# Two float32 blocks on one Trainium2 core: the high and low parts of the weights become slices of one tensor that begin 16 bytes into it, and every SBUF tensor behind them starts 32 bytes later

## What is computed

```
def swiglu(h, w_in, w_out):
    gate, up = jnp.split(h @ w_in, 2, axis=-1)
    return (jax.nn.silu(gate) * up) @ w_out
...
px = modulate(rms_norm(x, g_pre_mix[layer]), sh_m, sc_m) @ w_in[layer]
pc = modulate(rms_norm(ctx, g_pre_mix[layer]), csh_m, csc_m) @ w_in[layer]
...
mix_x = jnp.concatenate([att_x, ml_x], axis=-1) @ w_out[layer]
...
h = h + 0.5 * swiglu_2(rmsnorm(h, ffn1_norm[l]), ffn1_w_gate[l], ffn1_w_up[l], ffn1_w_down[l])
u = rmsnorm(h, mix_norm[l])
(aq, ak, av, gq, gk, gv, gr, g_low, gate_a, gate_b) = jnp.split(u @ w_in[l], offsets, axis=-1)
```

## The kernel before, in words

| operand | read by | start, mod 256 |
|---|---|---|
| `hi`, `lo` (any tile) | all large products | 0 |
| `mixH`, `mixL`, any k, 256 columns | `wout` (L2397), `bra`, `brb`, `wout2`, `gu2` | 192 |
| `g_high`, `g_low`, 256 columns | `dn0`, `dn2` | 192 |
| `g_high`, `g_low`, 272 columns | `dn1` | 192, 0, 64, 128 in turn with k |
| `n_high`, `n_low`, 258 columns | `gu0` | 192 |
| `n_high`, `n_low`, 272 columns | `gu1`, part of `in2k` | 192 |
| `n_high`, `n_low`, the 256 frames behind the 16 meta tokens | rest of `in2k`, `in2g` | 0 |
| `n5H`, `n5L`, 256 columns (L2133) | first block's projections | 128 |
| `row1` (weights of L2071, 2 moving columns) | modulation vectors | 224 |

## Time and profile before

### The profile page before, as it was taken

One profiled execution on the slowest core, in us unless ns is written; L12 is line 12 of the kernel. 1 busy time (PEld: TensorE's weight loads), 2 busy tenths in 40 slices (PEclk: granted clock), 3 DMA queues, 4 the chain that ended last, 5 costly groups with the idle time before them and its releaser, 6 DMA issues.

```text
span 963.9 us, 19405 instructions
## 1 busy us (share of the span) xinstructions
PE 950.4 (99%) x7543; PEld 882.2 (92%) x7543; DVE 639.9 (66%) x990; ACT 494.6 (51%) x762; POOL 69.1 (7%) x100
## 2 busy tenths in 40 slices
PE   8999999999999999999999999999999999999997
PEld 3776778899999999899999999999998999999997
DVE  4888886687666675765555546665777766666554
ACT  3765647655444544554444434644566555454531
POOL 0012002200000021000000000200120100000000
PEclk9999999999999999999999999999999999999999
DMA  9972437547556795266666744663345557667741
GB/s 361 400 259 89 132 132 242 164 166 216 174 176 183 206 320 158 68 197 175 180 181 179 222 118 127 211 191 110 111 131 163 167 156 235 193 197 210 218 142 44
DMA packets 189183, 176.06 MB, mean 183 GB/s; under 512 B 7312, under 2 KB 177824, under 8 KB 188752
## 3 DMA queue, kind: packets, MB, share of 16 engines
q1 hardware_dynamic: 183456, 154.29, 53.3%
q0 software_dynamic: 4960, 17.64, 5.2%
q10 hardware_dynamic: 720, 3.49, 0.9%
HBM read 174.32 MB, written 1.05 MB: 182 GB/s over the span
## 4 chain that ended last, share of the span: by engine, by line
PE 91%; DVE 6%; ACT 2%; issue 1%; POOL 0%; DVEq 0%; ACTq 0%; POOLq 0%
PE acc L2004 24%; PE acc L2006 24%; PE acc L2005 24%; PE acc L2397 2%; PE acc L2100 1%; PE acc L2202 1%; PE acc L2204 1%; PE acc L2203 1%; PE wk L2063 1%; PE wk L2004 1%; PE acc L2133 1%; PE wk L2006 1%; PE wk L2005 1%; DVE lo L1142 1%; PE wk L2701 1%
## 5 line engine op out<-in xcount | busy, mean ns | idle before, releaser
L1142 DVE TENSOR_TENSOR lo<-raw,hi 128x1024 fp32r<-128x1024 f32 (+1 forms) x259 | 330.9, 1288 | 205.7 <-ACT hi L620 205.4
L620 ACT ACTIVATE hi<-raw 128x1024 fp32r<-128x1024 f32 (+1 forms) x260 | 283.2, 1099 | 126.0 <-PE acc L2006 120.4
L2004 PE MATMUL acc<-n_high,hi 128*128 128x272 f32 (+3 forms) x1016 | 292.1, 288 | 0.4 <-DVE hbuf L1670 0.4
L2005 PE MATMUL acc<-n_low,hi 128*128 128x272 f32 (+3 forms) x1016 | 289.1, 285 | 0.0
L2006 PE MATMUL acc<-n_high,lo 128*128 128x272 f32 (+3 forms) x1016 | 289.1, 285 | 0.0
L2004 PEld LDWEIGHTS acc<-n_high,hi 128*128 128x128 f32 (+1 forms) x1016 | 192.2, 189 | 2.8 <-issue 1.4
L2005 PEld LDWEIGHTS acc<-n_low,hi 128*128 128x128 f32 (+1 forms) x1016 | 192.3, 189 | 0.5
L2006 PEld LDWEIGHTS acc<-n_high,lo 128*128 128x128 f32 (+1 forms) x1016 | 192.2, 189 | 0.2
L2004 PE MATMUL acc<-g_high,hi 128*128 128x256 f32 (+1 forms) x528 | 148.4, 281 | 0.0
L2006 PE MATMUL acc<-g_high,lo 128*128 128x256 f32 (+1 forms) x528 | 148.1, 281 | 0.0
L2005 PE MATMUL acc<-g_low,hi 128*128 128x256 f32 (+1 forms) x528 | 147.9, 280 | 0.0
(11 more groups left out here) (424 smaller groups left out, 1248.9 us busy)
## 6 DMA issues: line engine op xcount, KB each, us to landing
raw<-in_w_in SPq DMA_DIRECT2D x52, 512.0 KB, 3.9
raw<-in_w_ffn_in SPq DMA_DIRECT2D x44, 512.0 KB, 4.0
raw<-in_ffn_w_gate SPq DMA_DIRECT2D x44, 512.0 KB, 3.8
raw<-in_ffn_w_up SPq DMA_DIRECT2D x44, 512.0 KB, 3.8
raw<-in_ffn_w_down SPq DMA_DIRECT2D x32, 704.0 KB, 4.6
stage<-in_w_late POOLq DMA_DIRECT2D x24, 512.0 KB, 4.9
raw<-in_w_ffn_out SPq DMA_DIRECT2D x16, 704.0 KB, 5.8
raw<-in_w_out SPq DMA_DIRECT2D x16, 512.0 KB, 3.8
```

Source lines behind the costliest of these rows:

```text
L620: act.activation(hi[:, j, 0:width], raw[:, j, 0:width], ACT.Copy).then_inc(hi_ready, 1)
L1142: dve.tensor_tensor(lo[:, j, 0:width], raw[:, j, 0:width], hi[:, j, 0:width].bitcast(F32), ALU.subtract).then_inc(lo_ready, 1)
L2004: pe.matmul(out_, wH, xH, start=start, stop=False)
L2005: pe.matmul(out_, wH, xL, start=False, stop=False)
```

## The change

`hi` and `lo` are no longer two tensors. One tensor `split` of 2 x 4 x 1408 + 8 float32 (45088 bytes) takes their place, and `hi` and `lo` are views of it that leave 4 elements (16 bytes) free at its start and 4 at its end:

```
-        hi = sbuf(root, "hi", [P, RING, SLOT], F32R)
-        lo = sbuf(root, "lo", [P, RING, SLOT], F32R)
+        split = sbuf(root, "split", [P, 2 * RING * SLOT + 8], F32R)
+        hi, lo = (split[:, 4 + n * RING * SLOT:4 + (n + 1) * RING * SLOT].rearrange("p (j w) -> p j w", j=RING) for n in range(2))
```

## The result

The changed kernel took 981.06 us (median of 4 runs; 977.49 to 985.74), the kernel before beside it 969.48 us (median of 4 runs; 965.49 to 973.77). The ratio is 1.013, with a 95% interval of 1.0094 to 1.0166: slower by about 12 us. The forecast was 980 us. The profiled execution took 984.56 us, its span 982.8.

What follows compares the result with a forecast made beforehand. TensorE, busy 99% of the span, was taken to bound the kernel through the distance between matmul starts. The 967.4 us median plus 12.5 us for 2496 matmuls, all else zero, gave 980 us; 8-in-10 range 952 to 992.

Steps and rivals of the forecast that it cites:

- What bounds the kernel: Whole kernel: time is the number of matmuls times the distance between starts; the change acts only through that distance.
- (a): ACT and DVE accesses to hi and lo start 16 bytes later, some transfers 32: counted at nothing, hidden behind TensorE.
- (b): Large products: moving operands start 32 bytes later, weights 16; 2496 matmuls lose 5 ns each, 12.5 us (0 to 20).
- The row chosen for the price: Price per matmul for the 256-column groups at 192: taken from n5L, 281 against 276 ns, so +5 ns.
- the likeness with 258 columns: Moving operands: 256 columns from 224 touch 17 pieces of 64 bytes, as 258 columns do; at worst +8 ns.
- the comparison of rows 3 and 4: Equal-width matmuls by moving start mod 256: 276 to 277 ns at 192, 283 at 0, 281 at 128.
- (c): Weight loads, starting at 16 instead of 0: no change taken, with 7 ns for each load kept as a rival.
- The step beside it: Weight loads at 256 columns: the load, 112 ns, is slower than the stream, 107 ns, so its delay is seen in full.
- The other groups unchanged: 258 and 272 columns, dn1 and the frames: no change taken, at most 19.7 us to be won.
- the first rival: 258- and 272-column groups, dn1 and frames relieved: faster, 957.5 us for half, 948 for all; chance 0.25.
- The third case: Whole kernel: 16 bytes are too few to matter, or loss and relief cancel; 967 us, chance 0.31.
- Two reads, not independent: TensorE: moving stream and next weights read SBUF at once and slow each other by address; 276 against 283 ns.

Runs made afterwards that it cites:

- e2: The kernel before with all addresses slid 32 bytes down, so the distance between operands stays 192: 967.60 us, ratio 1.0006.
- e4: The changed kernel run again with no edit, for a second profile and more times: 978.04 us.
- e1: The changed kernel with all addresses slid 32 bytes down, so the distance between operands stays 208: 977.52 us, ratio 1.0122.
- e3: The kernel before with everything behind the weights starting 32 bytes later, weights left at 0, distance 224: 976.11 us, ratio 1.0096.
- e10: The kernel before with n_high and n_low 64 bytes earlier and a 64-byte pad ahead of g_high, putting the frames at distance 192: 973.12 us, ratio 1.0036.
- e11: The kernel before with a second view of n_high and n_low, 192 bytes later, for in2k, in2g and wout2 only: 965.55 us, ratio 0.9994.

## Why the prediction was right, and where its reasons were not

**What bounds the kernel: right.** PE ends last in all stages, no new wait appeared, and only the distance of starts changed.

**(a), the copies and transfers at nothing: right.** ACT's 260 copies took a mean of 1099 ns before and after. Sliding all addresses (e2) cost nothing.

**(b), the groups at 192 lose: right in sign and place, its size low for the profiled run.** Forecast were 2496 matmuls and 5 ns, 12.5 us. Measured were 8.6 ns for `mixH` and 7.1 for `g_high`, 19.9 us, in the first profile, and 4.8 and 6.9 ns, 14.2 us, in e4's. The time of the kernel in 4 runs lay 12 us up. That the 980 us forecast and the median of 981.06 agree within 1 us is partly luck: the four times are 977.5 twice, 984.56 and 985.74, and by the rhythms that the stages took its two profiles differ by 6.7 us, of which the prediction knew nothing. The row chosen for the price, `n5L` at distance 128, was a good neighbour: at seven of the ten other distances 256 columns take 118.0 to 119.8 ns, 4.7 to 6.5 above 113.3; at 32 and 48 they take 116.9, at 208 one of two values. The step that failed is the reason given beside it, the likeness with 258 columns that touch a seventeenth piece of 64 bytes. e1 and e2 refute it: off and on multiples of 64 the times are the same. What counts is the distance, as the comparison of rows 3 and 4 had it.

**(c), the load itself at zero: right as far as tested.** e3 leaves the weights at 0 and is nearly as slow, 976.1 us against 978.0 and 981.1. L2071, where hardly anything moves beside the loads, has a median of 251 ns for each matmul in both kernels. The step beside it, that a load takes 112 ns and so sets the pace at 256 columns, is not shown. L2253, whose matmuls have 128 columns and a full weight load each, has (0.82 - 0.27)/5 = 0.110 us from start to start in the kernel before; its loads last 141 ns and those of L2071 192 (medians), so the two need not be alike.

```profile
111.02 0.82 PE L2253 MATMUL wk<-cst,Sm 128*128 128x128 f32 x6
111.02 0.69 PEld L2253 LDWEIGHTS wk<-cst,Sm 128*128 128x128 f32 x6
```

**The other groups unchanged: nearly.** 258 columns +0.4 ns, 272 +0.8 to 1.0, `dn1` -0.4, frames -1.4: together 0.1 to 0.4 us. The frames' duration moved by 3 ns, 1 more than the sign given for them allowed. The relief that the first rival wanted came for the frames, 1.1 us, and for `dn1`, 0.2 us, against the 9.9 to 19.7 us of its price. The third case, both streams shifted too little to matter, is refuted with it; 16 bytes of distance matter, a common shift of both operands by 32 bytes does not.

**Two reads, not independent.** The Trainium skill ("TensorE: Matmul & The Clock Gate", the step-by-step of a matmul) has the next weight load take nothing from the running matmul. Eleven distances give for one shape 113.3 to 123.3 ns at full clock. So the trace does not agree: where the two operands lie to each other sets how fast the pair goes. By what means stays open; no run looked into the memory itself.

## What to carry to other kernels

Where TensorE streams 256 to 272 float32r columns and loads a new stationary tile beside each, try the distance between the two operands' SBUF addresses mod 256 as a parameter of its own: here it is worth 1.0 to 1.5% of the kernel. A shift of both operands by the same amount leaves the distance alone (32 bytes were tested, at no cost), while any change between them that is not a multiple of 256 alters it. Count matmuls in equal windows, stage by stage, rather than compare medians: a stage can settle in one of two rhythms 4% apart. A gain under 1% that rests on one profile may be only that, and an edit that helps one stage can come with the slower rhythm in another, as in e10 and e11.

## What the runs showed of the hardware that was not expected

- A stage of equal matmuls settles in one of two rhythms and keeps it for hundreds of them: 113.3 or 117.8 ns at distance 192, 117.8 or 123.3 (alternately 117 and 130) at 208, with identical instructions and a granted clock of 1.00. A rhythm can also change within a stage: `dn0` of the kernel before begins at 117.8 ns in both profiles and is at 113.3 some 10 us later. What decides was not found.
- With a full weight load between, two starts stand 113.3 ns apart at 256 columns and distance 192, 112 at L2071's 2 columns, and 109 to 110 at L2253's 128. So 128 or 254 columns fewer save only 1 to 4 ns. That something in the load sets this floor was not tested.
- 272 columns depend on the distance in another order than 256 (best at 192 and 160, worst at 176 and 128), and 258 columns in a third (best at 160 and 224). No distance is best for all shapes: 192 is it for 256 columns and, with 160, for 272, but 258 columns take 0.8 ns less at 160 and 224.
